# Block 2 of a four-layer network: probabilities and state output turned by VectorE's 32x32 transposes and a trip through memory instead of by TensorE

## What is computed

```python
h = h + 0.5 * swiglu(rmsnorm(h, ffn1_norm), ...)
z = rmsnorm(h, mix_norm) @ w_in            # 4096 + 8 + 1024 + 512 + 2048 columns
m_qk = silu(causal_dwconv(m_qk, m_conv_w, m_conv_b))
hm = sigmoid(m_o) * head_rmsnorm(mlstm_chunkwise(mq, mk, mv, ig, lf), m_out_norm)   # 4 heads of 256
ha = swa_gqa_sinks(aq, ak, av, a_sinks)    # 16 query heads of 64, 4 key heads, window of 128
merged = sigmoid(g_m) * (hm @ w_branch_m) + sigmoid(g_a) * (ha @ w_branch_a)
h = h + merged @ w_out
h = h + 0.5 * swiglu(rmsnorm(h, ffn2_norm), ...)
h = h + sigmoid(rmsnorm(h, ple_norm) @ ple_gate_w) * (p_i @ ple_proj_w)
```

## Time and profile before

| what | value |
|---|---|
| executions | 2297.91, 2291.97, 2290.42 us (median 2291.97) |
| profiled execution, its own time | 2293.15 us |
| its span, first to last instruction | 2291.4 us |
| granted TensorE clock over the span | 1.00 |
| busy: PE, PEld, DVE, ACT, POOL | 2278.3, 1902.6, 1533.0, 1232.8, 134.6 us |
| moved by the core's DMA engines | 483.08 MB, 62.8% of 16 engines' span on SyncE's queue |

### The profile page before, as it was taken

One profiled execution on the slowest core, in us unless ns is written; L12 is line 12 of the kernel. 1 busy time (PEld: TensorE's weight loads), 2 busy tenths in 40 slices (PEclk: granted clock), 3 DMA queues, 4 the chain that ended last, 5 costly groups with the idle time before them and its releaser, 6 DMA issues.

```text
span 2291.4 us, 30120 instructions
## 1 busy us (share of the span) xinstructions
PE 2278.3 (99%) x11144; PEld 1902.6 (83%) x11144; DVE 1533.0 (67%) x2411; ACT 1232.8 (54%) x1890; POOL 134.6 (6%) x141
## 2 busy tenths in 40 slices
PE   9999999999999999999999999999999999999999
PEld 8887888888888888888888888888888888888887
DVE  6667786566687866676487666664765687657654
ACT  6556444445555444355467754554544477645443
POOL 3140000013220000000000000000000000000000
PEclk9999999999999999999999999999999999999999
DMA  8556568756485587487564444875677564456772
GB/s 337 197 181 257 192 230 293 225 184 211 148 293 192 184 278 240 164 274 248 188 232 154 165 153 160 270 244 195 220 239 239 180 221 157 148 175 204 233 238 87
DMA packets 179857, 483.08 MB, mean 211 GB/s; under 512 B 20480, under 2 KB 65152, under 8 KB 178688
## 3 DMA queue, kind: packets, MB, share of 16 engines
q1 hardware_dynamic: 179712, 481.16, 62.8%
HBM read 452.24 MB, written 28.84 MB: 210 GB/s over the span
## 4 chain that ended last, share of the span: by engine, by line
PE 94%; DVE 3%; DMA 1%; ACT 1%; issue 1%; SPq 0%; DVEq 0%; ACTq 0%
PE bank L2113 28%; PE bank L2118 27%; PE bank L2117 27%; PE bank L2160 2%; PE bank L2100 2%; PE bank L2101 2%; PE bank L2102 2%; DMA raw<-in_weights 1%; DVE wl L1602 1%; PE bank L2249 1%; PE bank L2211 0%; PE bank L2182 0%; PE bank L2234 0%; ACT wh L1372 0%; SPq L1190 0%
## 5 line engine op out<-in xcount | busy, mean ns | idle before, releaser
L1372 ACT ACTIVATE wh<-raw 128x1024 fp32r<-128x1024 f32 (+1 forms) x778 | 813.6, 1051 | 774.7 <-PE bank L2118 684.1
L1602 DVE TENSOR_TENSOR wl<-raw,wh 128x1024 fp32r<-128x1024 f32 (+1 forms) x778 | 932.7, 1229 | 271.0 <-ACT wh L1372 267.8
L2113 PE MATMUL bank<-wh,xh 128*128 128x512 f32 (+1 forms) x2102 | 825.8, 393 | 5.3 <-issue 4.0
L2118 PE MATMUL bank<-wh,xl 128*128 128x512 f32 (+1 forms) x2102 | 815.9, 388 | 0.0
L2117 PE MATMUL bank<-wl,xh 128*128 128x512 f32 (+1 forms) x2102 | 814.9, 388 | 0.0
L2113 PEld LDWEIGHTS bank<-wh,xh 128*128 128x128 f32 x2102 | 394.7, 188 | 86.9 <-issue 7.8
L2118 PEld LDWEIGHTS bank<-wh,xl 128*128 128x128 f32 x2102 | 394.5, 188 | 81.1
L2117 PEld LDWEIGHTS bank<-wl,xh 128*128 128x128 f32 x2102 | 394.9, 188 | 77.1
L2113 PE MATMUL bank<-wh,act_h 128*128 128x512 f32 x528 | 205.9, 390 | 0.0
L2118 PE MATMUL bank<-wh,act_l 128*128 128x512 f32 x512 | 199.3, 389 | 0.0
L2117 PE MATMUL bank<-wl,act_h 128*128 128x512 f32 x512 | 199.3, 389 | 0.0
(11 more groups left out here) (347 smaller groups left out, 2068.5 us busy)
## 6 DMA issues: line engine op xcount, KB each, us to landing
raw<-in_weights SPq DMA_DIRECT2D x760, 512.0 KB, 4.3
turn<-ffn_s SPq DMA_DIRECT2D x264, 64.0 KB, 2.8
ffn_a<-turn SPq DMA_DIRECT2D x66, 256.0 KB, 4.6
raw<-in_weights SPq DMA_DIRECT2D x16, 384.0 KB, 3.4
ln<-in_ln SPq DMA_DIRECT2D x4, 1024.0 KB, 7.5
moved<-merged SPq DMA_DIRECT2D x32, 128.0 KB, 6.6
merged<-moved SPq DMA_DIRECT2D x8, 512.0 KB, 5.3
bias<-in_bias SPq DMA_DIRECT2D x2, 1024.0 KB, 8.6
```

The source lines that it names most:

```text
L1372: act.activation(wh[:, u % NH, 0:used(u)], raw[:, u % NR, 0:used(u)], ACT.Copy).then_inc(hi_done, 1)
L1602: dve.tensor_tensor(wl[:, u % NR, 0:used(u)], raw[:, u % NR, 0:used(u)], wh[:, u % NH, 0:used(u)].bitcast(F32), ALU.subtract).then_inc(lo_ ...
L2113: pe.matmul(out, h, w_h, start=st.first and i == 0, stop=False)
L2118: last = pe.matmul(out, lo, w_h, start=False, stop=ends)
```

## The change

Each pair's probabilities go through memory: one 32x32 transpose of 128x768 on VectorE, four writes, one read, and the product reads the result as it has landed, without a copy. The `mo` output goes the same way in two halves. `heads` is no longer used for block 2; each pair has a start place (`PAIRS_AT`) and offsets from it (`PAIR_STEPS`). `aq1`'s block and out move from before the narrow unit to the side list (block 4, out 5, back 7, copy 10). `a_sum` goes from place 1 to 2 and 3. Sorted, the pairs' scores stand at 6, 9, 12, 16, 19, 22, 26, 29 and the products at 15, 18, 21, 25, 28, 31, 35, 38, each alone; `m_rows` at 33 (38 before), `m_fin` at 44 (49), block of `mo` 45, out 46 and 47, back 48 and 49, halve 52 and 53. Tables now give places directly and may reorder; for block 1 the places are the old ones, but for 16 side steps from the differential attention's first scores on, which stand one unit later (da scores 39 to 40, and so on).

```diff
-UNITS_AMONG_2 = "100110300011211002110001101011110011110401001111100100111101101000101020040102"
+PLACES_2 = (1, 2, 3, 2, 3, 4, 5, 7, 10, 6, 8, 6, 8, 9, 9, 10, 11, 12, 12, 12, 13, 14, 15, 15, 15, 16, 16, 18, 18, 18,
...
+PAIRS_AT = (6, 9, 12, 16, 19, 22, 26, 29)
+PAIR_STEPS = (("pv", 9), ("back", 6), ("even", 2), ("s", 0), ("block", 3), ("out", 4))
...
-    for name in ("ak", "aq0", "aq1"):
-        if name == "aq1":
-            p.moved("back", name)
-        c_a = p.moved("copy", name)
+    for name in ("ak", "aq0"):
+        p.moved("copy", name)
+    for what in ("block", "out", "back", "copy"):
+        c_a = p.moved(what, "aq1", kept=q["aq1"])
...
-    q["o"] = heads(p, "aa", AH // 2, scores, q["akv"])
+    for _, _, what, pair in sorted((at + after, k, what, pair) for pair, at in enumerate(PAIRS_AT)
+                                   for k, (what, after) in enumerate(PAIR_STEPS)):
...
+        elif what == "block":
+            p.moved("block", f"pair{pair}", h=h, m=evens[pair])
+        elif what in ("out", "back"):
+            p.moved(what, f"pair{pair}", h=h)
...
-    t_m = split_rows("mo", "hm", KT, rows=p.cc["rows"])
+    for what in ("block", "out", "back", "halve"):
+        for r in range(R):
+            h_m = p.moved(what, f"mo{r}", rows=p.cc["rows"], dst="hm", tile=r)
...
+        for i in range(AH // 2):
+            stage[f"pair{i}"] = (flat[:, 0:768], flat[:, 768:1536], b["PT"][:, :, :].rearrange("p a n -> p (a n)"))[i % 3]
...
+                    elif k == "block" and st.name.startswith("pair"):
+                        dve.wait_ge(evened, st.m)
+                        dve.transpose(stage[st.name].rearrange("p (q m n) -> p q m n", q=4, m=6),
+                                      b["Pn"][:, st.h % 4:st.h % 4 + 2, :].rearrange("p a n -> p (a n)")
+                                      .rearrange("p (m q n) -> p q m n", m=6, q=4)).then_inc(blocked, 1)
...
-                        turned(st.t)
+                        if k == "ca_pv":
+                            turned(st.t)
+                        else:
+                            pe.wait_ge(moved_back[st.name], 16 * (st.l + 1))
...
+                            pairs = landed[st.name].rearrange("p (b m n) -> p m b n", b=4, m=6)
+                            sides = [(out, pairs[:, 3 * i:3 * i + 3], vs) for i, (out, pt, vs) in enumerate(sides)]
```

More of the change, by code:

```diff
@@ L169, in begin, with weave @@
         return kept
[L171 to L184, removed]
-        self.steps = before
[L186 to L192, removed]
+    def weave(self, before, dense, side, places):
+        assert len(places) == len(side), (len(places), len(side))
+        self.steps = before
+        left = sorted(zip(places, side), key=lambda pair: pair[0])
+        done = 0
+        for st in dense:
+            if st.kind == "unit":
+                while left and left[0][0] <= done:
+                    self.steps.append(left.pop(0)[1])
+                assert not any(sd.t is not None and sd.t == st.after_t for _, sd in left), st.u
+                assert not any(sd.kind == "o_split" and sd.o + 1 == st.after_o for _, sd in left), st.u
+                done += 1
+            self.steps.append(st)
+        self.steps += [sd for _, sd in left]
     def flip(self):
@@ L474, in plan_block1 @@
         merge(1, j, "w_branch_b", "ob", 4, j, ob_o + 1)
-    p.weave(before, dense_a + p.begin(), side, UNITS_AMONG_1)
+    p.weave(before, dense_a + p.begin(), side, PLACES_1)
     kept = p.begin()
@@ L735, in scores @@
         return p.count("soft"), p.count("soft")
-    q["o"] = heads(p, "aa", AH // 2, scores, q["akv"])
+    done, evens = {}, {}
+    for _, _, what, pair in sorted((at + after, k, what, pair) for pair, at in enumerate(PAIRS_AT)
+                                   for k, (what, after) in enumerate(PAIR_STEPS)):
+        h = 2 * pair
+        if what == "s":
+            done[h] = scores(h)[1]
+        elif what == "even":
+            evens[pair] = p.count("even", 2)
+            p.add("even", h=h, of="aa", soft=done[h], m=p.count("shares"))
+        elif what == "block":
[3 more added lines that the diff above has]
+        else:
+            if h % 4 == 0:
+                q["o"] = p.next_o()
+            p.add("aa_pv", h=h, o=q["o"], name=f"pair{pair}", kept=q["akv"])
+            if h % 4 == 2:
+                p.add("o_split", h=h, o=q["o"], dst="ha", n=p.count("hi"), m=p.count("o_ready_0"))
     p.add("m_rows", s=p.next_s())
@@ L760, in plan_block2 @@
     g_m = [gate2("hm", 5640, j, c_a[j]) for j in range(2)]
-    p.weave(before, dense_a + p.begin(), side, UNITS_AMONG_2)
+    p.weave(before, dense_a + p.begin(), side, PLACES_2)
     kept = p.begin()
```

58 lines of the change are left out of this document (32 added, 26 removed), and 3 rows, old and new, of the table PLACES_2.

## The result

The changed kernel takes 2320.27 us in the median (2319.22 to 2322.48, four executions); the kernel before, on the same chip, 2293.05 us (2290.42 to 2297.91, four). The ratio is 1.0117, 95% interval 1.0102 to 1.0132: **27 us slower**, where 13 us faster was forecast. Its profiled execution has a span of 2320.8 us.

A forecast was written before the change was run, and what follows sets the result against it. TensorE was taken as the bound, busy 2278.3 of 2291.4 us. The terms -10.6 - 3.5 + 1.7 - 1.1 + 0.9 = -12.6 us, set on the median, gave 2279.4, say 2280 us; range 2271 to 2288.

The forecast's parts named there:

- Transposes removed: TensorE, block 2: 96 transposes of Pn gone, -10.6 us, and 32 of mo, -3.5 us, in both layers.
- Products and scores apart: TensorE, pairs: eight scores and eight products each alone instead of mostly joined; +1.7 us in two layers, between 0 and 2.5.
- rival (d): Products on TensorE: the operand in runs of 32 is read at half pace, +2 us, 2294 us; 3%.
- Block 1: Differential attention: its scores move one unit later, so TensorE's wait for the turned keys goes; -1.1 us, once in two layers.
- The head: Start of block 2's mixing stage: waits of 2.6 us a layer where 2.1 were; +0.9 us in both layers.
- upper bound of +7.7: Start of the mixing stage: slower landings make the first pair's read-back 3.4 us late, 0.9 + 2 x 3.4.
- The prediction's own sign of being wrong: TensorE's read-back waits exceed 6 us a layer, or gaps at the mixing stage's start differ by over 3 us a layer.
- Nine units of a pair: Pairs, scores to product: the chain through memory takes 27.7 us, fits its 30.7 us window with 3 to spare, costs nothing.
- Rival (c): Pairs: product waits for its read-back, chain 5 us over its window as VectorE's and SyncE's queues add lag; 2309 us, 7%.
- Other queues: VectorE gets 9.7 us more a layer, hidden at 83% busy in the pairs' stretch; SyncE's and DMA's added work covered or hidden.
- The clock: TensorE's granted clock is 1.00 throughout, 2.4 GHz; a few us of waiting did not lower it.
- mo: mo through memory: ready 31.8 us after its last product's start, wanted at 34.2; 2.4 us of cover.

The follow-up runs named there:

- the last version: Kernel before with mo alone through memory, m_rows and row steps four units earlier, place 18's transposes kept ahead of the even step: 2294.29 us against 2294.18 (0.9999).
- The double and quarter runs: Changed kernel with each pair's VectorE transpose done twice: 2327.52 us; with only one of its four parts done: 2316.90 us.
- The trip alone: Kernel before with the first six pairs of eight through memory: 2306.93 us (+10.2); with only the third to sixth pair: 2302.43 us (+5.7).

## Why the prediction was wrong

What left TensorE's queue was, as far as the runs can tell, counted rightly (-14.1). The steps that failed are those that price what the moves do to VectorE's and ScalarE's queues: the head at +0.9 us (measured about +10 by itself), the m part's move, which has no term in the sum (12 us come back with two of its five units), and VectorE's added work, put at nothing as "hidden" (some 6 us by estimate). In their place the runs showed VectorE late at maxima, banks and `a_rows`, ScalarE standing behind it, and TensorE behind both.

**Transposes removed (-14.1).** The counts are right (96 transposes of Pn left, none of `mo`), and nothing contradicts their price: `mo`'s 32 back on TensorE measured 2.6 us against 3.5, inside the interval. As far as the runs can tell the term was right, and was paid for elsewhere.

**Products and scores apart (+1.7), the operand (0).** Right: 1.00 for a product that reads runs of 32 (0.95 forecast), so rival (d) is out.

**Block 1 (-1.1).** No gain seen: the stage began 1.96 us later than before (1177.08 against 1175.12), where 1.1 earlier was forecast. The wait for `kT` is gone, but 1.2 us (twice 0.6) appeared for VectorE's mixed probabilities, `Pn`. It was not tested by itself, and in the later profiles with block 1 unshifted the same matmul starts anywhere from 1173.6 to 1178.7; no cause is claimed.

**The head (+0.9).** This step failed: it measured about +10. Its gap of 0.3 was right (0.39), and so was a wait before the third chunk's banks (1.7 forecast, 1.0 found). The count went "through in order" for VectorE only, and for VectorE it was right: it had the first scores read out at 1205.5, and they were at 1207.6 in a trace whose stage starts 1.96 us later. But it never walked ScalarE's queue, where the keep of `mv0` stands behind the exponentials, and these behind the maxima (ready at 1209.2). That gave 3.3 us a layer and half clock behind. The upper bound of +7.7 stood for another event, a late read-back. The prediction's own sign of being wrong did not come: the gaps (0.2, 3.3 and 1.0 us) sum to 4.6 against 2.6, less than 3 apart, and the read-backs stayed under 6 us a layer. The signs looked at waits that the count already had.

**Nine units of a pair.** Fourteen of the sixteen read-backs came in time, and the wait forecast for "the first pair" in the upper bound came at the second, 1.9 and 2.6 us. Rival (c), which named this as the slower case, had the sign but hardly the mechanism: 4.5 us of the 27. What it did name, VectorE's queue adding its lag, is what the rows show; it strikes mostly at maxima and banks and not at the read-back.

**The m part: the step that was missing.** The prediction moved the m part to make room for `mo`'s trip, has no term for the move, and never asked when VectorE has `a_rows` at place 34 instead of 39. 13.8 us of waiting and the half clock behind it; 12 us by the run that moved it back by two units. The move does not cost this by itself: in the last version m_rows and the row steps stand four units earlier than before, with all pairs turned by TensorE, and no wait for `a_rows` is left; with two pairs through memory and the steps three units earlier it is 1.6 us a layer. It is the early step together with VectorE's lag.

**Other queues ("+9.7 us, hidden").** VectorE's share in the pairs' stretch was put at 83%, and taken as cover. Measured it is 76% (106.9 of 140 us, 1190 to 1330), since the waits lengthened the stretch. The double and quarter runs price its time at 0.4 us a us. An engine at that share that has ScalarE waiting for it in order, and waits for ScalarE itself, was no cover. What the prediction said of SyncE held by these rows, though its waits were longer: ScalarE waited for weight loads 7.2 us in the first layer's stage (1.1 before), but 1.3 with six pairs through memory, a kernel that lost 10 us, and 11.3 in the last version, which lost nothing. By these rows loads held back are not what costs the time.

**The clock.** "A few us of waiting did not lower it" was read from waits of 2.1 us at most and carried over to all. Beside 13.4 us a layer of added waits, TensorE's busy time holds 6.5 more than the count of its work gives, 4.6 of them counted in the first layer between matmuls, mostly at 1.2 GHz.

**mo.** Right: cover of 2.4 us forecast; the low part was done at 1385.4 and wanted at 1388.3, 2.9. But this cover had been bought with the m part's five units, and on the kernel before, where those are not free, the gain of 3.5 us did not show (+0.1, half-width 2).

The Trainium skill's page "VectorE: DVE Perf Modes", section "Rules for kernel authors", which the prediction set against the change, would have given the right sign: it keeps full transposes on TensorE where PSUM will do. The trip alone (+10.2 and +5.7) agrees with it.

**What the parts sum to.** They do not add: the head is worth 9 and the row steps 12, both together with one product moved 15. What of the remaining 12 over the kernel before belongs to VectorE's time, what to the order within the trip and what to tighter places stays open.

## What to carry to other kernels

Walk every engine's list past each moved step, also where the move seems only to make room: ask when each operand is made by its engine, not when its own step stands. When engines walk one list in order, price an addition to one of them by what stands behind it on the engine that waits for it; a busy share below 100% (76% here) is not cover by itself. And a stall of TensorE of some us can cost more than its length, here up to half as much again.

## What was not expected of the hardware

The same wait can leave the clock alone or halve it. In one execution of the last version the head's wait of 2.0 us stands in both layers:

```profile
1190.41 0.47 PE L2150 MATMUL bank<-wh,xh 128*128 128x512 f32 x1 [1.97 <-issue]
...
1854.46 0.47 PE L2150 MATMUL bank<-wh,xh 128*128 128x512 f32 x1 [1.96 <-issue]
```

```profile
1188.00:1198.00 10.00, 8.03 (x32) 6.13 (x32) 9.75 (x16) 5.80 (x8) 0.00 (x0) 0.83 0.49 181
1851.00:1861.00 10.00, 8.04 (x46) 6.46 (x44) 9.72 (x17) 7.40 (x9) 0.00 (x0) 1.00 0.65 237
```

Behind the first the granted clock is 0.83 over 10 us, 1.2 GHz in part and about 1.6 us lost by the distances of starts; behind the second it stays at 2.4 GHz. Of the changed kernel's waits, 1.9, 3.3 and 6.9 us were followed by the lower level, and one of 2.0 us behind the fifth product was not. What decides between them no run here shows.
